# First products of three stages from unnormalised activations, and two norms from one pass of row sums

## What is computed

```
def rmsnorm(x, g):
    y = x * rsqrt(mean(x * x, axis=-1) + EPS)
    return y * g

h = x + gmlp_mixer(rmsnorm(x, a_norm_g))            # two projections, spatial gating, product "go"
h = h + conv_ffn(rmsnorm(h, f_norm_g[0]))           # f0: 1024 -> 5632, causal conv, silu gate, 2816 -> 1024
kv = rmsnorm(h, kv_norm_g) @ w_kv                   # att: two norms of the same h
h = h + chunk_attention(rmsnorm(h, b_norm_g), kv)   # ends in product "wo"
h = h + conv_ffn(rmsnorm(h, f_norm_g[1]))           # f1
x = rmsnorm(h, final_norm_g)                        # end of the first block
n1 = rms_norm(x, norm1_g) * (1 + scale) + shift     # second block, scale and shift from the vector c
```

## Time and profile before

| | before |
|---|---|
| median of 3 runs | 2899.09 us (2898.22 to 2900.95) |
| the profiled execution | 2897.96 us, span 2896.2 us |
| mean granted TensorE clock | 0.966 |
| PE busy | 2681.4 us, 93% of the span |
| DVE, ACT, POOL busy | 879.6, 547.8, 448.1 us |
| HBM traffic | 147 GB/s over the span |

### The profile page before, as it was taken

The page is one execution under the profiler, slowest core; times in us unless marked ns, Lnnn a source line. Parts: engine busy times, 40 slices in busy tenths (PEclk is TensorE's granted clock), DMA queues, the critical chain, the costliest instruction groups (busy, mean ns, idle before and its releaser), DMA issues. The chain is left out here.

```text
span 2896.2 us, 27277 instructions
## 1 busy us (share of the span) xinstructions
PE 2681.4 (93%) x9949; PEld 1395.8 (48%) x9949; DVE 879.6 (30%) x1927; ACT 547.8 (19%) x1039; POOL 448.1 (15%) x385
## 2 busy tenths in 40 slices
PE   6998999999999999999969989999988999999992
PEld 5543444444565544444424546567645544444440
DVE  2024222201332232221032335556633322222225
ACT  1201111100233211110023552222112111111111
POOL 3004555410000100000013101011110111111110
PEclk8998999999999999999989999999998999999996
DMA  8223455422211222223213111000114599999985
GB/s 170 73 66 108 145 150 152 143 80 62 59 52 51 66 71 74 72 75 92 80 30 102 52 33 48 25 15 15 37 75 158 213 399 416 407 403 395 391 357 213
DMA packets 290830, 407.23 MB, mean 141 GB/s; under 512 B 14258, under 2 KB 253560, under 8 KB 264608
## 3 DMA queue, kind: packets, MB, share of 16 engines
q1 hardware_dynamic: 274048, 366.46, 36.3%
q0 software_dynamic: 16112, 37.19, 4.4%
q10 hardware_dynamic: 560, 2.10, 0.2%
HBM read 396.20 MB, written 30.46 MB: 147 GB/s over the span
## 5 line engine op out<-in xcount | busy, mean ns | idle before, releaser
L878 PE MATMUL bank<-hT,bring 128*128 128x512 f32 x1408 | 617.8, 599 | 16.0 <-DVE hT L1883 16.0
L878 PEld LDWEIGHTS bank<-hT,bring 128*128 128x128 f32 x1408 | 267.6, 192 | 349.3 <-issue 336.7
L844 PE MATMUL bank<-bring 128*128 128x512 f32 x704 | 303.0, 592 | 0.0
L1478 PE MATMUL bank<-bring 128*64 128x512 f32 (+1 forms) x512 | 227.0, 596 | 1.9 <-issue 1.0
L649 POOL TENSOR_TENSOR ysq<-ysq 128x512 f32<-128x512 f32 x36 | 47.1, 1307 | 1092.2 <-ACT ysq L1549 1090.7
L844 PEld LDWEIGHTS bank<-bring 128*128 128x128 f32 x704 | 133.5, 190 | 166.9 <-issue 166.7
L1906 DVE SCALAR_TENSOR_TENSOR ffw<-bank,col,ffw 128x511 f32<-128x511 f32 x88 | 66.0, 750 | 433.1 <-ACT ffw L1572 433.1
L1572 ACT ACTIVATE ffw<-bank,col 128x512 f32<-128x512 f32 x88 | 68.5, 778 | 520.7 <-PE bank L878 520.7
L1891 DVE TENSOR_TENSOR xT<-bank,xT 128x512 f32<-128x512 f32 x32 | 22.1, 692 | 378.5 <-PE bank L844 378.5
L1478 PEld LDWEIGHTS bank<-bring 128*64 128x64 f32 (+1 forms) x512 | 77.8, 157 | 97.4 <-issue 96.2
L1491 PE MATMUL bank<-bring,xT 128*64 128x512 f32 (+1 forms) x256 | 116.9, 599 | 5.5 <-DMA ysq<-exp_w_down 3.2
(11 more groups left out here) (428 smaller groups left out, 3585.4 us busy)
## 6 DMA issues: line engine op xcount, KB each, us to landing
bring<-f_w_in SPq DMA_DIRECT2D x88, 512.0 KB, 4.9
bring<-exp_w_gate SPq DMA_DIRECT2D x32, 1024.0 KB, 11.0
bring<-exp_w_up SPq DMA_DIRECT2D x32, 1024.0 KB, 19.8
bring<-exp_w_down SPq DMA_DIRECT2D x32, 1024.0 KB, 21.8
two<-ada_w SPq DMA_DIRECT2D x24, 1024.0 KB, 7.9
bring<-f_w_down SPq DMA_DIRECT2D x16, 1408.0 KB, 6.9
two<-exp_w_gate SPq DMA_DIRECT2D x16, 1024.0 KB
two<-exp_w_up SPq DMA_DIRECT2D x16, 1024.0 KB
```

Source lines behind the costliest of these rows:

```text
L844: mm = pe.matmul(ps[BANKS[stage][n % 4]][:], w[:, k, n % per * P:(n % per + 1) * P], rhs[:, k, :], start=(k == 0), stop=(k == kb - 1))
L878: mm = pe.matmul(ps[2 * j + b][:], w[:, k, b * P:(b + 1) * P], hT[:, k, :], start=(k == 0), stop=(k == KB - 1))
L1478: mm = pe.matmul(ps[3][m * h:m * h + m, :].rearrange("p (m n) -> p m n", m=2), hgT[par][:, k, m * h:m * h + m], w, start=(k == 0), stop=(k ...
```

## The change

Ahead of f0, att and f1 the first two blocks of the next product no longer wait for the norm. ACT writes, behind each square, the block of xT times the gain alone (L1606 of the changed kernel; into yT for f0, into yT and hT for att, into gT for f1). PE's `raw_products` runs banks 0 and 1 from these, with the two steps of `mean_squares` between steps 1 and 2, and the last step of each bank at the end. DVE multiplies the two finished banks in place by rstd (`scale_raw`), behind the scaled blocks. In att the key's norm is scaled first, the query's behind the two banks. Slot j = 0 of f0's first step has no ada unit; every unit moves one slot on, and unit 21 into "f0dn"; POOL begins them after f0's norm.

Ahead of the second block the two norms come from one pass. With s the mean of x squared and g the final gain, the second norm needs the mean of (x g)^2 / (s + eps); ACT squares x and x g of each block as it is added, POOL sums both, and PE sums both over features into two columns per group of 128 tokens. The column for n1 is eps * (s + eps) + mean((x g)^2), whose root takes the place of both roots. One reciprocal on 128x8 follows, PE spreads the rows over banks 3 and 4, and DVE scales hT from bank 3 (with the product of both gains) and then xT from bank 4. POOL gets five memsets more at the start. Some semaphores are merged (decay and lora ones into side_act, side_step), and the small DVE steps for `gmod` and `qn8` move up to f1.

```diff
@@ POOL
+            porder(pool.memset(plain_w[:, 0:1], EPS / D))
+            porder(pool.memset(plain_w[:, 1:2], 1.0 / D))
+            porder(pool.memset(gained_w[:, 0:1], 1.0 / D))
+            porder(pool.memset(gained_w[:, 1:2], 0.0))
+            porder(pool.memset(eps_sq, EPS * EPS))
...
             square_sums("f0")
-            pool.wait_ge(s("col_ready"), len(PARAM_ROWS) + 1)
+            pool.wait_ge(s("norm_h_ready"), h_count("f0", KB - 1))
...
-            for n in ("att", "f1", "fin", "n1"):
+            for n in ("att", "f1"):
                 square_sums(n)
+            for b in range(1, KB - 1):
...
+                nc.gpsimd.tensor_tensor(sq[:, 0, :], sq[:, 0, :], sq[:, b, :], ALU.add)
+                nc.gpsimd.tensor_tensor(yT[:, 0, :], yT[:, 0, :], yT[:, b, :], ALU.add).then_inc(s("norm_sum"), 1)
@@ PE
+            def raw_products(n, before, freed):
...
+                for m in range(2):
+                    pe.wait_ge(s("lin_added"), plan[before][6] + freed + m + 1)
+                    for k in range(KB - 1):
+                        if m == 0 or len(RAW[n]) == 2:
+                            pe.wait_ge(s("raw_ready"), raw_count(n, k, m))
+                        product(m, k)
+                        if m == 0 and k == 1:
+                            mean_squares(n)
+                for m in range(2):
+                    if m == 0 or len(RAW[n]) == 2:
+                        pe.wait_ge(s("raw_ready"), raw_count(n, KB - 1, m))
+                    product(m, KB - 1)
...
-                        if l == 0:
-                            ada_unit(2 * i + j, j)
+                        if l == 0 and not (first and j == 0):
+                            ada_unit(2 * i + j - 1, 1 - j)
...
-            mean_squares("fin")
-
-            mean_squares("n1")
+            pe.wait_ge(s("norm_sum"), 6 * (nth("n1") - 1))
+            pe.wait_ge(s("norm_sq_ready"), KB * nth("n1"))
+            for t in range(TT):
+                for b, src, w in ((0, sq, plain_w), (0, yT, gained_w), (KB - 1, sq, plain_w), (KB - 1, yT, gained_w)):
+                    mm = pe.matmul(ps[7][:, 2 * t:2 * t + 2], src[:, b, t * P:(t + 1) * P], w, start=(b == 0 and src is sq),
+                                   stop=(b > 0 and src is yT))
+            mm.then_inc(s("norm_ss_ready"), 1)
+            pe.wait_ge(s("row_inv"), 1)
+            for m in range(2):
+                for t in range(TT):
+                    mm = pe.matmul(ps[3 + m][:, t * P:(t + 1) * P], row_inv[:, 4 * m + t:4 * m + t + 1].to_broadcast([P, P]),
+                                   ident[:], start=True, stop=True)
+                mm.then_inc(s("row_spread"), 1)
@@ ACT
                     nc.scalar.activation(sq[:, b, :], xT[:, b, :], ACT.Square).then_inc(s("norm_sq_ready"), 1)
+                    for dst, gain in RAW[n] if n in RAW else ():
+                        nc.scalar.activation(dst[:, b, :], xT[:, b, :], ACT.Identity, scale=col[:, gain + b:gain + b + 1])\
+                            .then_inc(s("raw_ready"), 1)
@@ DVE
+            def scale_raw(n, used, base):
+                for m in range(2):
+                    dve.wait_ge(s(used), base + m + 1)
+                    nc.vector.tensor_tensor(ps[m][:], ps[m][:], rstd[:], ALU.mult).then_inc(s("raw_scaled"), 1)
...
-            normalise("att", [(hT, C_B), (gT, C_KV)])
+            normalise("att", [(gT, C_KV)])
+            scale_raw("att", "qkv_prod", 0)
+            scaled_blocks(hT, C_B)
```

More of the change, by code:

```diff
@@ L862, in linear, with product @@
                         ada_unit(between[n], between[n] % 2)
+            def raw_products(n, before, freed):
+                used = {"f0": "ff_prod", "att": "qkv_prod", "f1": "ff_prod"}[n]
+                def product(m, k):
+                    mm = pe.matmul(ps[m][:], slot(0, 8, 256)[:, k, m * P:(m + 1) * P], RAW[n][m % len(RAW[n])][0][:, k, :],
+                                   start=(k == 0), stop=(k == KB - 1))
+                    if k == KB - 1:
+                        mm.then_inc(s(used), 1)
+                for m in range(2):
[10 more added lines that the diff above has]
+                    product(m, KB - 1)
             def feed_forward(l):
@@ L870, in body @@
                         w = slot(j, 8, 256)
+                        if first and j == 0:
+                            raw_products(f"f{l}", ("go", "wo")[l], 4)
                         for b in range(2):
+                            if first and j == 0:
+                                continue
                             if not first:
@@ L1018, in att_fill @@
                 if i + 1 < PAIRS:
-                    projection(i + 1, min(qt, 2), HALVES[half] if qt < 2 else range(4 * (qt - 2) + 2 * half, 4 * (qt - 2) + 2 * half + 2))
+                    projection(i + 1, min(qt, 2), HALVES[half] if qt < 2 else range(4 * (qt - 2) + 2 * half, 4 * (qt - 2) + 2 * half + 2),
+                               g == 0)
                 else:
@@ L1024, in att_fill @@
                         linear_step("wo", yT, KB, n, k)
-            for m in range(3):
-                projection(0, m, range(KB), True)
+            ring_ready(pe, "att", 0, 0)
+            raw_products("att", "f0dn", 6)
+            pe.wait_ge(s("norm_h_ready"), h_count("att", KB - 1))
+            projection(0, 2, range(KB))
             att_scores(0)
@@ L1567, in body @@
                             settle(act_e, s("ff_prod"), 44 * l + 4 * i + 2 * j + b + 1)
+                            if first and j == 0:
+                                act_e.wait_ge(s("raw_scaled"), scaled_count(f"f{l}", b))
                             if not first:
@@ L1875, in _, with scaled_blocks @@
             order = Order(dve, s("dve_order"))
+            def scaled_blocks(dst, gain):
+                for b in range(KB):
+                    nc.vector.scalar_tensor_tensor(out=dst[:, b, :], in0=xT[:, b, :],
+                                                   scalar=col[:, gain + b:gain + b + 1], in1=rstd[:],
+                                                   op0=ALU.mult, op1=ALU.mult).then_inc(s("norm_h_ready"), 1)
             def normalise(n, outs):
```

139 lines of the change are left out of this document (80 added, 59 removed).

## The result

The changed kernel takes **2845.96 us** (median of four runs, 2842.95 to 2847.23), the kernel before 2898.65 us beside it (2895.92 to 2900.95): a ratio of 0.9817, 95% interval 0.9801 to 0.9832. The forecast was 2846.0 us in a range of 2842 to 2853. The agreement is closer than the steps deserve: one was 2.7 us too good, and others made it up.

The account below looks back on a forecast made before the run. PE, with work for 93% of the span, was taken as the bound. Gains 17.9 + 8.9 + 8.2 + 18.9 less 0.9 make 53.0 us; 2897.96 becomes 2845.0, plus 1.1 for the median: 2846.0 us, range 2842 to 2853.

Parts of the forecast that it names:

- E: In each of the four norms, the moment the product ahead hands over to the first mean matmul; times count from it.
- The three covers: Raw stages f0, att, f1: scaled blocks ready before PE asks for them, by 2.3, 1.6 and about 2.3 us.
- Rival 2: Raw stages: cover thinner than counted, each stage waits 1 to 2 us, 2849 to 2852 us; chance 0.07.
- 32 in 3.8: Double norm: PE's 32 sum instructions take 3.8 us, scaled from a row of 8 in 0.95.
- So 8 in 0.9: Double norm: PE's spread to bank 3, 8 instructions, takes 0.9 us, from a row of 64 in 7.24.
- rival 1: PE's small products do not keep the clock up: 4.7 us at most, 2850.7, or 2853.2 with the start's fall; chance 0.13.
- 9.36: Double norm: favw's 16 instructions keep their old 9.36 us, against 6.86 at full pace.
- the sigmoid ends at 19.8: Double norm: favw's sigmoid ends 19.8 us behind E, after DVE's xT blocks at 19.0; fox starts at 21.3.
- next in line: Double norm: DVE's scaling of xT is 0.8 us behind becoming the bound; with quick favw it holds fox at 20.6.
- 20.6 - 6.3: Double norm, from E: fox start at 20.6 us if DVE holds it, less the sums' end with hand-over at 6.3.
- Rival 3: A later stage, the experts' weight streaming, catches up; a loss of a third of the gain gives 2864 us; chance 0.03.
- Rivals 4 and 5: 4: ring loads behind ada loads in SP's queue, slower kernel, 0.03; 5: raw products still wait for norms, 2881 us, 0.03.

Follow-up runs that it names:

- thin_att: Changed kernel with six spare ACT copies ahead of the root of att's norm: 2845.24 us, ratio 0.9818.
- ada_gate_only: Kernel before with one line changed, so POOL starts the ada units only after f0's eight scaled blocks: 2885.48 us, ratio 0.9952.
- warm: Changed kernel with two spare matmuls behind the last down product, ahead of the double norm's sums: 2847.36 us, ratio 0.9813.
- busy_sums: Changed kernel with warm's two spare matmuls and one more of 512 columns behind each group of eight sums: 2844.45 us, ratio 0.9817.
- late_consts: Changed kernel with POOL's five memsets moved behind the issue of the bias's reload: 2842.74 us, ratio 0.9811.
- fox_early: Changed kernel; PE waits for the decay gate only at the keys' sums, POOL takes the first head's rows before storing the running sum: 2840.59 us, ratio 0.9794.
- raw_no_gate: Changed kernel with POOL's ada units free to start as before, not waiting for f0's scaled blocks: 2855.88 us, ratio 0.9852.
- fox_best: Changed kernel with the edits of fox_early and late_consts together: 2838.97 us, ratio 0.9794.

## Why the prediction was right, and where it was not

**The three raw stages: right to a tenth.** Forecast 17.9, 8.9 and 8.2 us, measured 17.92, 8.88 and 8.14. The rule that carried them was counting PE's steps at full pace: if nothing waits, the end of the stage is 18 steps behind E whatever the other engines do. The three covers were put at 2.3, 1.6 and about 2.3 us and measured 2.3, 1.9 and 2.3 between DVE's eighth block and PE's first use. Rival 2 did not happen, and thin_att shows how near it is: 3.2 us more on ACT bring it about. I had held the old DVE time of 17.79 us to be POOL's doing by comparing it with a stage without POOL; ada_gate_only shows it.

**The double norm: the mechanism right, the sum mis-sized.** Forecast 18.9 us, measured 16.20 in the pair, and 16.0 to 18.6 over the five profiles of this code. The term that failed is "32 in 3.8": I took the pace of eight small instructions that stood between dense products, at full clock, for 32 that stand alone. They took 6.58 us, all but the first 0.4 at a granted 0.50. "So 8 in 0.9" for the spread's first bank failed by the same reason: both banks take 3.60 us where they take 2.05 at full clock. That is rival 1, which I gave 0.13. Its total did not come about, because the other term was mis-sized the other way: favw took 7.03 us and not 9.36, as the clock had come back by then.

And "the sigmoid ends at 19.8", ahead of which xT was to be done with 0.8 us to spare, turned round: with the sums and the spread late but favw fast, DVE became the gate. I had named that as next in line. The 15.18 us from the end of the sums to fox say the same: they hold with favw at 7.03 us and at 7.94 (warm). At full clock, in busy_sums, they are 14.3, which is the prediction's own DVE chain, 20.6 - 6.3. So the loss against the forecast is the low clock in the sums (about 2.6 us) and in the spread (0.9), less the 0.7 by which the forecast had let favw hold fox longer than DVE.

**The start: not to be told.** I charged 0.9 us for five memsets; in the pair of profiles PE was 0.92 us earlier. Both are below what the wait for the bias does by itself: between 1.1 and 5.5 us at the first GELU in the nine profiles with the memsets in the same place. The mean of E(f0) is 229.2 us over the nine profiles with the memsets ahead and 228.2 over the two without (before, ada_gate_only) as over the two with them behind. That is the size I charged, but in a scatter of 4.5 us it shows nothing. Only POOL's own 0.7 us are shown (late_consts).

**From fox to the end: nothing given back.** Rival 3 would have made the last column longer by a third of the gain, 17 us; it is 1.06 longer in the pair and scatters over 9 whatever was edited. Rivals 4 and 5 did not happen: no ring load makes L925 wait, and the raw steps ran without one; the 1 MB ada loads even land in 5.3 us (median) where it was 7.9.

**The closeness of 2846.0 to 2845.96** is the sum of an error of 2.7 us in the double norm, 1.1 us of fox to end and 1.8 us of luck at the start, and of the medians against the profiled executions (51.0 us between the two spans, 52.7 between the medians). So the hit to a tenth is luck, and the range was the honest part. (The sum as written gives 2899.09 - 53.0 = 2846.1, put down as 2846.0.)

## What to carry to other kernels

Work on an unnormalised input with the factor put in afterwards pays the wait and the low clock behind it, here 8 to 9 us for a wait of 5; count the steps until the first consumer of the scaled form and give the chain of the other engines less than that. Before restructuring, look for the cheap half: holding POOL back alone gave 9.6 us of f0's 17.9. And a hand-over that waits for a side result ahead of dense work can cost twice, by the wait and by the clock behind it, so wait where the result is used (fox_early: 3.4 us of wait, and up to 3 us of clock that the end of the run did not show).

## What the runs showed of the hardware that I had not expected

**Small products do not keep TensorE's clock up.** Behind E, PE has an idle time of 2.15 us, then the 32 instructions of 2 columns without a pause. The granted clock fell to 0.50 in each of the nine profiles that had the small ones alone, 2.5 to 5.4 us behind E, also in warm with an idle time of 0.43; with a matmul of 512 columns behind each eight it stayed at 1.00. But the small products are not the only cause. In raw_no_gate the fall came 0.2 us behind the start of the first of them (at 1452.43), when PE had done little else than stand idle since E (1450.12):

```profile
1450.10:1451.10 1.00, 0.18 (x1) 0.00 (x0) 0.69 (x1) 0.06 (x1) 0.00 (x0) 1.00 0.00 0
1451.10:1452.10 1.00, 0.00 (x0) 0.00 (x0) 0.00 (x0) 1.00 (x2) 0.00 (x0) 1.00 0.55 126
1452.10:1453.10 1.00, 0.67 (x4) 0.70 (x5) 0.00 (x0) 0.98 (x2) 0.00 (x0) 0.76 1.13 341
1453.10:1454.10 1.00, 1.00 (x6) 1.00 (x6) 0.00 (x0) 0.69 (x2) 0.00 (x0) 0.50 1.18 320
```

So the idle time can bring the fall about and the small products can too, nearly without it; in both cases the clock stayed low through sums and spread. Sums with no idle time at all ahead of them were not run. The same code took 6.58 us and 4.15:

```profile
1450.86 4.15 PE L1089 MATMUL bank<-small,ysq 128*128 128x2 f32 x32 [2.15 <-ACT ysq L1714]
```

This is thin_att, where the fall came 1.1 us before their end; its two stretches below lie on either side. The Trainium skill (TensorE: Matmul & The Clock Gate, What's actually happening) says of the rise of the clock that its moment depends on where in a free-running window the first matmul lands. It says so of the rise only; that the fall scatters between equal code here agrees with a window of that kind, and does not show it.

```profile
1448.60:1453.00 4.40, 2.25 (x21) 2.17 (x20) 0.69 (x1) 2.73 (x4) 0.00 (x0) 1.00 0.76 199
1454.50:1460.50 6.00, 5.19 (x21) 4.17 (x21) 2.78 (x5) 2.21 (x5) 0.00 (x0) 0.50 0.00 0
```

**Whole stages that nobody edited scatter, and the clock with them.** The 20 us that begin 720 us behind the first fox product had a granted clock of 0.91 in raw_no_gate and 1.00 in fox_early:

```profile
2194.40:2214.40 20.00, 16.64 (x74) 9.79 (x72) 10.53 (x30) 0.00 (x0) 1.12 (x1) 0.91 0.08 22
```

```profile
2187.50:2207.50 20.00, 15.87 (x98) 11.62 (x97) 7.30 (x25) 5.09 (x10) 3.29 (x4) 1.00 0.39 122
```

The two are out of step by then (72 and 97 weight loads), so only their clocks compare. All thirteen profiles fall into two sets by this stretch: six with 1.00 there take 1371.3 to 1372.8 us from fox to the end (ada_gate_only, fox_early, thin_att, busy_sums, late_consts, fox_best), seven with 0.91 take 1376.2 to 1380.0 (the others, before and after among them). A granted 0.91 over 20 us costs less than 2 us, so this stretch is a mark of the set and not the whole difference of 3.4 to 8.7 us. What decides which set a run falls into was not tried. An edit of a microsecond can be read only in the segment that it touches.
